# Output projection's second half: two of eight tile pairs per layer as seven block products

## The reference, cut to what matters

```
mix = concat(out_a, out_b, out_c) @ w_out[l]     # (640 x 2048) @ (2048 x 2048)
x   = x + gate * mix                             # gate per output column, one set for latent, one for prompt tokens
```

## Time and profile before

| | |
|---|---|
| device time, median of 3 runs | 2118.82 us (2118.49 to 2120.38) |
| span of the profiled execution (its own time but for what lies around the span) | 2118.3 us |
| TensorE busy | 2084.8 us (98%) |
| VectorE busy | 1487.4 us (70%) |
| ScalarE busy | 646.9 us (31%) |
| GpSimd busy | 173.2 us (8%) |
| granted clock of TensorE, mean | 0.999 |

### The profile page before, as it was taken

The page is one execution under the profiler, slowest core; times in us unless marked ns, Lnnn a source line. Parts: engine busy times, 40 slices in busy tenths (PEclk is TensorE's granted clock), DMA queues, the critical chain, the costliest instruction groups (busy, mean ns, idle before and its releaser), DMA issues.

```text
span 2118.3 us, 33687 instructions
## 1 busy us (share of the span) xinstructions
PE 2084.8 (98%) x13031; PEld 1854.6 (88%) x13031; DVE 1487.4 (70%) x2921; ACT 646.9 (31%) x1100; POOL 173.2 (8%) x118
## 2 busy tenths in 40 slices
PE   5999999999999999999999999999999999999998
PEld 4788888888999999999998888888899999999998
DVE  5879789999666667866475455566666666677776
ACT  4232221311333334442043222232133333354312
POOL 0000000000000000523310000000000000043321
PEclk9999999999999999999999999999999999999999
DMA  9989687664333324664445647444343233266444
GB/s 365 388 303 341 211 282 261 233 222 161 115 106 104 106 71 130 201 208 142 128 129 166 189 127 216 144 143 146 109 128 107 74 101 107 86 213 214 149 120 154
DMA packets 357334, 365.43 MB, mean 173 GB/s; under 512 B 17670, under 2 KB 264156, under 8 KB 356572
## 3 DMA queue, kind: packets, MB, share of 16 engines
q1 hardware_dynamic: 328528, 320.67, 47.2%
q10 hardware_dynamic: 28684, 43.09, 5.4%
HBM read 304.98 MB, written 58.72 MB: 172 GB/s over the span
## 4 chain that ended last, share of the span: by engine, by line
PE 95%; DVE 2%; DMA 1%; issue 1%; ACT 0%; ACTq 0%; SPq 0%; DVEq 0%
PE psP L926 30%; PE psP L999 8%; PE psT L938 8%; PE psO L1008 7%; PE psP L996 6%; PE psP L994 6%; PE psP L995 6%; PE psP L1001 4%; PE psT L1008 4%; PE psP L1193 3%; PE psO L1239 3%; PE psT L1204 2%; PE psO L968 1%; DMA wmod<-in_w_mod_dram 1%; DVE r_a L2124 1%; PE psP L1056 1%
## 5 line engine op out<-in xcount | busy, mean ns | idle before, releaser
L926 PE MATMUL psP<-x_pair,high 128*128 128x512 f32 x1704 | 546.7, 391 | 0.0
L926 PEld LDWEIGHTS psP<-x_pair,high 128*128 128x128 f32 x1704 | 319.8, 188 | 70.5 <-issue 3.4
L926 PE MATMUL psP<-x_pair,low 128*128 128x512 f32 x852 | 331.8, 389 | 0.0
L1485 ACT ACTIVATE high<-raw 128x1024 fp32r<-128x1024 f32 x128 | 135.4, 1059 | 590.8 <-PE psT L938 504.2
L2025 DVE SCALAR_TENSOR_TENSOR macc<-mraw,cond,macc 128x128 f32<-128x128 f32 (+1 forms) x810 | 308.7, 455 | 0.0
L2043 DVE TENSOR_TENSOR low<-raw,high 128x1024 fp32r<-128x1024 f32 x128 | 157.1, 1228 | 172.9 <-ACT high L1485 172.8
L999 PE MATMUL psP<-x_pair,high 128*128 128x512 f32 x512 | 200.9, 392 | 0.0
L926 PEld LDWEIGHTS psP<-x_pair,low 128*128 128x128 f32 x852 | 160.0, 188 | 33.0 <-issue 0.5
L994 PE MATMUL psP<-x_pair,high 128*128 128x384 f32 x512 | 180.2, 352 | 0.0
L996 PE MATMUL psP<-x_pair,low 128*128 128x384 f32 x512 | 172.2, 336 | 0.0
L995 PE MATMUL psP<-x_pair,high 128*128 128x384 f32 x512 | 171.7, 335 | 0.0
(11 more groups left out here) (359 smaller groups left out, 4040.1 us busy)
## 6 DMA issues: line engine op xcount, KB each, us to landing
raw<-in_w_in_dram SPq DMA_DIRECT2D x132, 512.0 KB, 5.1
wmod<-in_w_mod_dram SPq DMA_DIRECT2D x32, 1024.0 KB, 8.6
mraw<-in_w_mod_dram SPq DMA_DIRECT2D x64, 512.0 KB, 4.2
mraw<-in_w_mod_dram SPq DMA_DIRECT2D x32, 1024.0 KB, 7.4
raw<-in_w_in_dram SPq DMA_DIRECT2D x32, 1024.0 KB, 5.5
raw<-in_w_out_dram SPq DMA_DIRECT2D x64, 512.0 KB, 4.0
old<-x_scratch SPq DMA_DIRECT2D x64, 320.0 KB, 2.9
xf<-proj_scratch SPq DMA_DIRECT2D x48, 320.0 KB, 3.3
```

The source lines that it names most:

```text
L926: mm = pe.matmul(latent_ps[m], own, moved, start=(k == 0 and w is whole and x is x_high), stop=(k == KT - 1 and x is x_low))
L1485: act.activation(ring(high, l, n), ring(raw, l, n), ACT.Copy).then_inc(s["chunk_cast"], 1)
```

## The change

Of the eight tile pairs of the second half, pairs 3 and 5 (output tiles 6, 7 and 10, 11) are computed in both layers by a two-by-two block scheme with seven products in place of eight. The blocks are: even and odd k-tiles, first and second 320 tokens, first and second tile of the pair. A product is 4 k-tiles x 3 parts, each a matmul of 128 x 128 weights over 320 tokens. The other six pairs ("plain") stay as they were.

New work is: four token sums per layer (1280 columns each; sum, rounding on ScalarE, remainder), four weight sums for each pair of the two (512 columns each), the rounding and remainder of seven weight blocks (512 columns each), and 13 VectorE instructions that join the seven products into x. The old x of those tiles is loaded straight into `xf` (`kept_in`). The loops of the second half are unrolled on SP, TensorE, ScalarE and VectorE. Several semaphores are shared by what used two before; this changes names and counts, not what is waited for.

The diff, cut to its core:

```diff
+SEVEN_PAIRS = (3, 5)
+PLAIN = [i for i in range(OUT_PAIRS) if i not in SEVEN_PAIRS]
+B11, B21, T2, T1, B22, T3, T4 = range(SEVEN)
+JOIN_OF = (0, 1, 2, 7, 4, 6, 10)
 # SP queue
+                quad_weights(0)
+                for n in range(1, PLAIN_PAIRS - 1):
+                    second_weights(1, n)
+                    sp.wait_ge(s["taken0"], n + occ + SECOND + SEED)
+                    old_x(0, PLAIN[n])
+                    second_weights(0, n + 1)
+                    sp.wait_ge(s["taken1"], n + occ + SECOND + SEED)
+                    old_x(1, PLAIN[n])
+                    if n == 2:
+                        kept_in(0)
+                        kept_in(1)
+                        quad_weights(1)
 # TensorE
+                def seventh(m, idx):
+                    q, out = m * SEVEN + idx, product_banks[idx]
+                    pe.wait_ge(s["block_split"], weights_split(l, q + 1))
+                    if idx in (B11, T4):
+                        pe.wait_ge(s[f"taken{idx // T4}"], occ + SECOND + SEVEN_PAIRS[m] - m + SEED)
+                    if m > 0 and 2 <= idx < T4:
+                        wait_joined(m - 1, idx)
...
+                    for k in range(QUAD):
+                        for w, x in ((whole, x_whole), (whole, x_rest), (rest, x_whole)):
+                            mm = pe.matmul(out, w[:, k, :], x[:, k, :], start=(k == 0 and w is whole and x is x_whole),
+                                           stop=(k == QUAD - 1 and w is rest))
 # ScalarE
+                for i in range(OUT_PAIRS - 1):
+                    if i == 0:
+                        token_cast(S1)
+                    if i == 1:
+                        token_cast(S2)
+                        token_cast(S4)
+                    if i == 2:
+                        token_cast(S3)
+                        for idx in range(4):
+                            quad_cast(idx)
+                    if i + 1 in SEVEN_PAIRS and i > 2:
+                        for idx in range(4):
+                            quad_cast(SEVEN * SEVEN_PAIRS.index(i + 1) + idx)
+                    if i in SEVEN_PAIRS:
+                        corner_copy(SEVEN_PAIRS.index(i))
+                    for slot in range(2):
+                        square(i, slot)
+                        if i + 1 in SEVEN_PAIRS:
+                            for idx in ((4, 5), (6,))[slot]:
+                                quad_cast(SEVEN * SEVEN_PAIRS.index(i + 1) + idx)
 # VectorE
+                def token_rest(idx):
+                    dve.wait_ge(s["block_cast"], tokens_split(l, TOKEN_SUMS[idx]))
+                    dve.tensor_tensor(token_low[idx][:], token_sum(idx), token_high[idx][:].bitcast(F32), ALU.subtract)\
+                        .then_inc(s["block_split"], 1)
...
+                split_plain(0, 1)
+                token_summed(S1)
+                add_plain(0, 0)
+                split_plain(1, 0)
+                token_rest(S1)
+                token_summed(S2)
+                add_plain(0, 1)
+                weigh_up_to(0)
+                split_plain(1, 1)
+                token_rest(S2)
+                token_summed(S4)
+                add_plain(1, 0)
+                weigh_up_to(1)
+                split_plain(2, 0)
+                token_rest(S4)
+                token_summed(S3)
+                sum_weights(0)
+                add_plain(1, 1)
+                weigh_up_to(2)
+                token_rest(S3)
+                split_plain(2, 1)
+                quad_rest(B11)
+                quad_rest(B21)
+                quad_summed(0, T2)
+                quad_summed(0, T4)
+                add_plain(2, 0)
+                weigh_up_to(3)
+                quad_rest(T2)
+                quad_rest(T1)
+                quad_rest(B22)
+                quad_rest(T3)
+                add_plain(2, 1)
+                weigh_up_to(4)
+                quad_rest(T4)
+                for idx in range(SEVEN):
+                    join(0, idx)
+                    if idx == T2:
+                        split_plain(3, 0)
+                    if idx == B22:
+                        weigh_up_to(5)
+                        split_plain(3, 1)
+                sum_weights(1)
+                quad_rest(SEVEN + B11)
+                quad_rest(SEVEN + B21)
+                quad_summed(1, T2)
+                quad_summed(1, T4)
+                add_plain(3, 0)
...
```

More of the change, by code:

```diff
@@ L1375, in _ @@
                 pe.wait_ge(s["g_out"], 2 * (l + 1) * PAIRS + SEED)
[L1376 to L1382, removed]
@@ new lines, in _ @@
+                for i in range(OUT_PAIRS):
+                    if i in SEVEN_PAIRS:
+                        for idx in range(SEVEN):
+                            seventh(SEVEN_PAIRS.index(i), idx)
+                        continue
+                    p = PLAIN.index(i)
+                    n = occ + SECOND + p
+                    for j in range(2):
+                        if i - 1 in SEVEN_PAIRS:
+                            m = SEVEN_PAIRS.index(i - 1)
+                            if j == 0:
+                                pe.wait_ge(s["corner_copied"], l * len(SEVEN_PAIRS) + m + 1)
+                            wait_joined(m, (B21, T4)[j])
+                        if i == OUT_PAIRS - 1 and j == 1:
+                            last_half_tile(2 * p + 1, psP[1], n)
+                        else:
+                            half_tile(2 * p + j, psP[j], n, (f"taken{j}", n + SEED),
+                                      l * KT + HALF_K if i == 0 and j == 0 else None)
@@ L2538, in finish_last @@
                         weigh_last(slice(LEFT, TOK)).then_inc(s["left_step"], 1)
-                def finish(i, last=False):
-                    for f in range(3 if last else 4):
-                        after = i * 2 + (f + 1) // 2
-                        split_half(f + 1, after + (occ + SECOND), after + (whole + OUT_PAIRS))
-                        add_product(lambda part: xf[:, bass.ds(i * 4 + f, 1), part].rearrange("p a b -> p (a b)"),
-                                    psP[f % 2], f, i * 4 + f, i * 2 + (f // 2 + occ + SECOND),
-                                    i * 2 + (f // 2 + l * KT + OUT_PAIRS), i * 8 + 2 * (l * (KT - 1) + f + 1))
-                        if l + 1 == DEPTH and f > 0:
-                            weigh(i * 4 + (f - 1))
-                    if last:
-                        finish_last()
-                    elif l + 1 == DEPTH:
-                        weigh(i * 4 + 3)
@@ new lines, in _ @@
+                quad_rest(SEVEN + T4)
+                for idx in range(SEVEN):
+                    join(1, idx)
+                    if idx == T2:
+                        split_plain(4, 0)
+                    if idx == B22:
+                        weigh_up_to(9)
+                        split_plain(4, 1)
+                split_plain(5, 0)
+                add_plain(4, 0)
+                weigh_up_to(10)
+                weigh_up_to(11)
+                split_plain(5, 1)
+                add_plain(4, 1)
```

350 lines of the change are left out of this document (264 added, 86 removed).

## The result

The changed kernel takes **2127.5 us** (median of 5 runs, 2125.4 to 2128.8) against 2118.5 us for the kernel before (5 runs on the same chip): ratio 1.0037, 95% interval 1.0026 to 1.0048. It is slower by 0.37%, more than the 0.2% that can be told from no change. The forecast was 2128.0 us, inside a range of 2115 to 2134.

A forecast was written before the change was run, and what follows sets the result against it. TensorE, busy 98% of the span, was taken as the bound: -6.2 + 5.25 + 6.65 + 0.1 + 3.4 = +9.2 on 2118.3 us gives 2127.5, plus 0.5 to the median: 2128.0 us, range 2115 to 2134.

The forecast's parts named there:

- Rival A: TensorE's stalls before tile 5 come as forecast but the clock stays: +5.8, 2124.6 us; chance 0.14.
- B: VectorE's list is shorter, GpSimd's adds mostly hidden: stalls 1.2 and 2.6 us, clock stays, 2116.4 us; chance 0.20.
- C: Tile 5's split is ready in time, needing 6.85 us less list; TensorE keeps its 6.2 us: 2112.6 us; chance 0.15.
- D: VectorE also bounds the seven-product pairs, 2 us at each except layer 0's first: +6 more, 2134 us; chance 0.05.
- E: Price goes by the matmul, not the column, so 84 for 80 save nothing: +15.4, 2134 us; chance 0.01.
- four pairs: TensorE, two pairs per layer: seven products take 12.32 us instead of 13.87, saving 1.55 us a pair, 6.2 us in all.
- wait before tile 5, layer 0: TensorE waits for tile 5's split on VectorE: 6.85 us of delays against 1.6 us spare, so 5.25 us.
- waits before tiles 4 and 5, layer 1: Layer 0's stall plus three more `weigh` on VectorE at 0.46 us each: 6.65 us, part already before tiles 3 and 4.
- clock behind tile 5: After TensorE's long idle time the clock falls to 1.2 GHz, losing 1.7 us per layer, 3.4 us; bounds zero and about twice.
- second seven, tile 9: Second seven-product pair and tile 9's late weights: nothing lost in layer 0, 0.1 us in layer 1.
- layer boundary: The layer's end keeps its distances, since two plain pairs follow the second seven-product pair; no loss was forecast.
- the wait for the cast: VectorE's last token remainder waits for ScalarE's cast, queued behind tile 3's square: 2.3 us with two handovers.

The follow-up runs named there:

- experiment 3: Changed kernel with GpSimd adding only one column of squares for tiles 0, 1 and 2 in both layers: 2117.5 us, ratio 0.9990 to the kernel before.
- experiment 2: Changed kernel with VectorE's split of tile 5 and add of tile 3 ahead of the first weight sums: 2121.4 us, ratio 1.0007 to the kernel before.
- stall_filled: Changed kernel with TensorE doing 18 (layer 1: 15) unread 512-column matmuls between tiles 4 and 5 instead of idling: 2122.6 us, ratio 1.0015.
- boundary_wide: Changed kernel with 5 filling products of 512 columns replacing 4 of 128 at the layer boundary: 2127.2 us, ratio 1.0028 to the kernel before.
- shifted: Changed kernel with 4 more unread 512-column products ahead of tile 14 in layer 0, moving the layer boundary later: 2127.3 us, ratio 1.0031.
- experiment 1: Changed kernel with ScalarE casting the last token sum (S3) ahead of tile 3's square: 2125.5 us, ratio 1.0027 to the kernel before.

## Why the prediction came out right, and where it was off

**The mechanism** was the forecast's in both layers, and no rival's. Rival A (clock stays) falls by the windows, B and C (VectorE in time, GpSimd hidden) by the waits of 4.8 and 4.1 us and by experiment 3, D (VectorE as the bound in the sevens) because TensorE's timeline has no wait there in the changed kernel, E (price by the matmul) by 12.31 us for 84 products. One figure of C was wrong: for tile 5 to be in time the list had to be 5.25 us shorter in layer 0, not 6.85, since 1.6 us were to spare. D's ingredients were there, though: experiment 2 shows them at 2.8 and 3.4 us once tile 5's stall doesn't cover them.

**The terms**, forecast and measured:

| term | forecast, us | measured, us |
|---|---|---|
| four pairs | -6.2 | -6.2 (13.87 - 12.31 each) |
| wait before tile 5, layer 0 | 5.25 | 4.92 |
| waits before tiles 4 and 5, layer 1 | 6.65 | 4.86 |
| clock behind tile 5 | 3.4 | 3.4 |
| second seven, tile 9 | 0.1 | none |
| layer boundary | none | 1.6 |

- *Layer 0.* The list from 979.26 to 1013.97 is 34.7 us long, against 28.3 + 6.85 = 35.15. GpSimd took 1.37 + 1.17 + 1.37 = 3.9 us (forecast 4.05) and another 0.36 from the fourth remainder, the wait for the cast 1.96 (2.3).
- *Layer 1 was mis-sized by 1.8 us.* The step that failed is "layer 1 has three more weigh in the list", added to layer 0's stall as if the rest were equal. VectorE's list starts 4.12 us behind tile 0 (1998.16 - 1994.04) and in layer 0 4.83, 0.7 less; GpSimd cost 1.38 + 1.25 + 1.25 = 3.9 us against 4.05 (2.87 and 2.48 us in the rows for 1.49 and 1.23); the wait for the cast was 1.51 us against the 2.3 forecast. These three are 1.7 of the 1.8 us.
- *The boundary* was taken to "keep its distances". From the last product of layer 0's stretch to the next layer's first it took 7.05 us (1088.97 to 1096.02) against 5.42 before (1085.93 to 1091.35): the third fall of the clock, which no step of the forecast had.
- *The clock.* The term came out at 3.4 us, but its ground was weaker than the forecast says. "The only idle stretch of that length and the clock fell" is one trace's answer: the same wait before the same matmul is in all eleven traces. In ten of them it lasts 2.77 us, and the clock fell behind it in three (the kernel before, stall_filled, boundary_wide) and stayed at 1.00 in seven, the changed kernel's own among them. (Two longer waits, 4.3 and 14.1 us, lie in the first 19 us, before TensorE had any stretch of work, and settle nothing here.)

```profile
46.02 0.47 PE L1058 MATMUL psP<-x_pair,high 128*128 128x512 f32 x1 [2.77 <-DVE x_pair L2276]
...
46.00:48.00 2.00, 1.99 (x9) 1.65 (x10) 1.97 (x4) 2.00 (x5) 0.00 (x0) 1.00 1.04 400
48.00:50.00 2.00, 2.00 (x37) 1.24 (x35) 1.97 (x3) 2.00 (x5) 0.00 (x0) 1.00 1.06 409
```

  In "shifted" that wait was 3.74 us and the clock fell. Behind the waits of 3.5 us and more at tile 5 it fell ten times out of ten, by 1.7 us seven times and by 3.4 us three times, which is the upper bound the forecast had set.
- *Against each other.* The terms measured sum to +8.6 us, the spans differ by 7.4. Tile 0 of layer 0 started 0.5 us earlier in this trace (974.43 against 974.90; over all eleven traces it starts at 972.89 to 975.61, whatever the kernel). Another 0.5 us is the kernel before's own: its first 14 tiles take 97.59 us in layer 1 (1989.54 to 2087.13) against 97.07 in layer 0 (974.90 to 1071.97), which the forecast's 6.935 us a tile leaves out. The two misses, -1.8 and +1.6, cancelled; that the time came within 0.5 us is in part luck.
- *The time around the span.* I took 0.5 us from span to median. In the changed kernel's runs each time is 1.8 us above its span (2127.5 and 2125.7), and so it is in later runs of the kernel before (2120.0 and 2118.2). By that its profiled execution took some 2120.1 us and was one of the slower ones of its kernel (2117.6 to 2120.4).

**The price by the column.** 12.31 us for 84 products of 320 columns is 0.147 us each, while 80 of 384, 256 and 512 columns (384 on average) take 13.87 us, 0.173 each. The Trainium skill, "TensorE: Matmul & The Clock Gate", section Back-to-back issue gap, gives a sustained 81 ns for 128 columns and 131 ns for 512, by which the cost would follow the number of matmuls more than their columns. The trace doesn't agree with that.

## What to carry to other kernels

Work that goes from the bound engine to one with room needs a list of due times, not an average load: here the same work was 0.37% slower in one order and 0.29% faster in another. In an engine that works in order, put what somebody waits for (splits, adds that free a bank) ahead of preparation that is due later, and do the same in each queue that feeds it, SP's loads too. A stall that is taken away uncovers what it hid, so look through the whole stretch before the order is called right.

## What was not expected of the hardware

- The clock's fall costs different amounts. Behind tile 5 of layer 0 in the run "shifted" the shares were 0.53, 0.50, 0.50 and 0.77 from 1014 to 1022, 3.4 us missing against 1.7 in the changed kernel, after the same wait of 4.76 us (part of it, before 1015.2, lies in the idle time itself). Layer 1 of "shifted" and of "boundary_wide" lost 3.4 us too:

```profile
1014.00:1016.00 2.00, 0.79 (x2) 0.79 (x3) 2.00 (x3) 0.00 (x0) 0.00 (x0) 0.53 0.84 205
1016.00:1018.00 2.00, 2.00 (x8) 1.90 (x8) 1.97 (x5) 1.00 (x2) 0.00 (x0) 0.50 0.30 123
1018.00:1020.00 2.00, 2.00 (x8) 1.81 (x7) 1.97 (x5) 0.86 (x3) 0.00 (x0) 0.50 0.80 225
1020.00:1022.00 2.00, 2.00 (x11) 1.95 (x10) 1.88 (x2) 1.07 (x3) 1.70 (x1) 0.77 0.25 102
```

- In the changed stretch idle times of TensorE of up to 1.8 us left the clock at 1.00, and those of 3.5 us and more were followed by the lower level. Between them length alone doesn't decide: after the same 2.77 us near the kernel's start the clock fell in three traces and stayed in seven.
- With no idle time but 0.3 us the clock fell at the layer boundary too, in both traces of one program and in none of the others.
- VectorE and GpSimd hold each other up both ways: GpSimd's add of 1.56 us took 2.35 us where it began inside a split of VectorE, and VectorE's next instruction 2.86 in place of 1.49. A cast, with one operand in SBUF to read, is held up as well: 2.02 us in place of 0.68 in experiment 1.
